# Convolution by halves of the tokens, gate products and half of the taps inside the attention, in a residual block with expert retrieval

## What is computed

```python
h = x @ w_in + b_in                # conv GLU 1024 | q, k, v 3 * 512 | gates 2 * 1024
a, gate = split(h_glu)             # branch A
c = a * sigmoid(gate)
c = causal_depthwise_conv(c, w_dw) + b_dw        # 31 taps, 512 channels
y_conv = silu(layer_norm(c)) @ w_pw2 + b_pw2
z = q @ k.T * scale                # branch B: 8 heads, strictly causal
suffix = reversed_cumsum(log_sigmoid(-z)) - log_sigmoid(-z)
y_sb = (exp(log_sigmoid(z) + suffix) @ v) @ w_o
mix = (sigmoid(g_A) * y_conv + sigmoid(g_B) * y_sb) @ w_out + b_out
x = layer_norm(alpha * x + mix)
# PEER, per token and head: two top-16 of 128 keys, top-16 of the 256 sums -> 16 expert rows
x = layer_norm(alpha * x + sum(gate * gelu(x . u[idx]) * v[idx]))
```

## Time and profile before

| | us |
|---|---|
| median of 3 runs (3281.8 to 3286.63) | 3284.27 |
| profiled execution | 3283.15 |
| its span | 3281.3 |
| first gather issued | 523.2 |
| PE, DVE, ACT, POOL busy | 2446.8, 2297.7, 1159.3, 1326.3 |
| mean granted clock of TensorE | 0.864 |

### The profile page before, as it was taken

How to read it: one execution, slowest core, us unless ns; L and a number is a source line. 1 busy time by engine, 2 the same in 40 slices (tenths; PEclk the granted TensorE clock), 3 DMA queues, 4 the chain that set the end, 5 groups by cost and what they waited for, 6 DMA issues and landing times. The chain is left out here.

```text
span 3281.3 us, 37294 instructions
## 1 busy us (share of the span) xinstructions
PE 2446.8 (75%) x12464; PEld 998.8 (30%) x12464; DVE 2297.7 (70%) x4704; ACT 1159.3 (35%) x3326; POOL 1326.3 (40%) x1197
## 2 busy tenths in 40 slices
PE   8987996778778777769899888885555555555555
PEld 7864653332223333323233332221111111111111
DVE  6986215776668888876667866666777677767775
ACT  3106112333334555533333333333333333333332
POOL 3400003344445544544343344444455445444553
PEclk9998997888888898889999999997777777777777
DMA  3101226999999999999999999999999999999997
GB/s 142 39 0 65 77 104 272 396 413 420 421 420 405 410 409 375 409 420 410 397 397 419 394 409 412 421 419 421 409 421 421 420 398 421 421 421 402 421 421 313
DMA packets 162792, 1163.71 MB, mean 355 GB/s; under 512 B 17857, under 2 KB 17985, under 8 KB 26178
## 3 DMA queue, kind: packets, MB, share of 16 engines
q0 software_dynamic: 147456, 1073.81, 79.7%
q1 hardware_dynamic: 15170, 87.79, 6.8%
HBM read 1157.33 MB, written 4.19 MB: 354 GB/s over the span
## 5 line engine op out<-in xcount | busy, mean ns | idle before, releaser
L809 PE MATMUL ps<-arena_high 64*64 64x512 f32 x8192 | 1275.3, 749 | 724.2 <-ACT arena_high L1163 721.2
L590 POOL DMA_INDIRECT arena_high<-uv_dram,idx_now x1024 | 1201.8, 1174 | 1468.7 <-PE ps L809 1269.4
L1486 DVE SCALAR_TENSOR_TENSOR arena_high<-arena_low,arena_high 128x1024 f32<-128x1024 f32 x1024 | 1237.2, 1224 | 631.4 <-DMA arena_high<-uv_dram,idx_now 620.8
L809 PEld LDWEIGHTS ps<-arena_high 64*64 64x64 f32 x8192 | 308.3, 156 | 1567.7 <-ACT arena_high L1163 1101.6
L1154 ACT ACTIVATE gcol<-hcol 128x2 f32<-128x2 f32 x512 | 103.7, 202 | 1405.8 <-DVE arena_high L1486 1403.7
L1163 ACT ACTIVATE arena_high<-arena_high,wcol 128x64 f32<-128x64 f32 x1024 | 300.4, 340 | 16.7
L1156 ACT ACTIVATE wcol<-gcol,arena_high 128x1 f32<-128x1 f32 x1024 | 245.7, 287 | 16.8
L778 PE MATMUL ps<-arena_low 128*128 128x512 f32 (+1 forms) x512 | 223.5, 580 | 0.0
L1331 DVE SCALAR_TENSOR_TENSOR arena_low<-arena_high,cols,arena_low 128x1024 f32<-128x1024 f32 x120 | 183.9, 1533 | 4.3
L585 POOL CAST idx_now<-arena_high 128x8 uint32<-128x8 f32 x128 | 59.0, 461 | 255.3 <-DVE arena_high L1472 254.7
L211 PE MATMUL ps<-x_hi_bytes,w_bytes 128*128 128x512 f32 x384 | 151.0, 393 | 0.0
(11 more groups left out here) (169 smaller groups left out, 2476.4 us busy)
## 6 DMA issues: line engine op xcount, KB each, us to landing
arena_low<-slabs_dram SPq DMA_DIRECT2D x21, 1152.0 KB
arena_high<-uv_dram,idx_now POOLq DMA_INDIRECT x1024
arena_high<-w_mix_dram SPq DMA_DIRECT2D x8, 1536.0 KB, 6.8
arena_low<-w_mix_dram SPq DMA_DIRECT2D x8, 1536.0 KB
arena_high<-w_proj_dram SPq DMA_DIRECT2D x16, 512.0 KB, 3.5
arena_high<-xT_dram SPq DMA_DIRECT2D x8, 512.0 KB, 7.7
arena_high<-w_out_dram SPq DMA_DIRECT2D x2, 2048.0 KB, 11.1
arena_high<-x_dram SPq DMA_DIRECT2D x8, 512.0 KB, 7.8
```

The costliest lines, as they stand in the source:

```text
L590: pool.indirect_dma_start(out=ring[:, s % RING, :], out_offset=None, in_=uv_d, in_offset=bass.IndirectOffsetOnAxis(ap=idx_now[:, s:s + 1], ...
L809: last = nc.tensor.matmul(ps[out_rows, bank, :], diag[rows, s % DIAGS, :], ring[rows, s % RING, cs], start=False, stop=False, skip_group_c ...
L1486: last = nc.vector.scalar_tensor_tensor(out=ring[:, s % RING, 0:D], in0=x1[c][:, j, :], scalar=1.0, in1=ring[:, s % RING, 0:D], op0=ALU.mu ...
```

## The change

Order of the projections: a and gate of all four `c`, then four q, then four k. The GLU product is split in two: the half used first goes to `conv_in`, the other with its 30 tokens of overlap is kept in `conv_in_late` for all four `c`. The taps of `h` = 1 follow at once, 512 wide; the 124 taps of `h` = 0 (`conv_tap`) stand in the attention, four behind each of the 32 `break_stick`. Mean, variance, root and swish are done per half: for `h` = 1 among the value blocks, for `h` = 0 between the branch products. Gate products (`gate_group`) stand in the attention, one of 24 matmuls in each unit, ahead of the unit's transposes; the scores of the next unit now stand behind these transposes; their sigmoids go to `mixT` and `gate_sb`. Subtraction of rounded gate weights moves from VectorE to GpSimd (`split_gates`), which does the first ahead of the attention and the other 14 in it. In the mix only branch products stay, over three pairs of PSUM banks; their weights and those of the gates are loaded apart. ScalarE rounds the value weights only when the fourth channel group's taps are done. The second half of `w_out` is loaded after the last mixed product, not the last branch product. Scores use two PSUM banks in place of four. Memory is laid out anew for all this (not shown). The core of the diff:

```diff
+            sp_eng.wait_ge(proj_done, 4 * CC)
+            load_gate(0)
+            sp_eng.wait_ge(var_done, 1)
+            load_gate(1)
             sp_eng.wait_ge(v_done, NB)
-            for m in range(2):
-                sp_eng.dma_start(w_mix[:, m, :], w_mix_d[m, :, :]).then_inc(wmix_in[m], 16)
+            load_branch(0)
+            load_branch(1)
+            for m in range(2, KD):
+                sp_eng.wait_ge(gates_done, 2 * m - 2)
+                load_gate(m)
+            sp_eng.wait_ge(gates_done, 2 * KD)
             sp_eng.dma_start(w_out_early[0], w_out_d[:, 0:CC, :]).then_inc(wout_in[0], 16)
-            for m in range(2, KD):
-                sp_eng.wait_ge(branch_done, m - 1)
-                sp_eng.dma_start(w_mix[:, m % 2, :], w_mix_d[m, :, :]).then_inc(wmix_in[m % 2], 16)
+            sp_eng.wait_ge(av_done, NU)
+            load_branch(2)
+            load_branch(3)
+            sp_eng.dma_start(b_out_bc[0], b_out_d.partition_broadcast(P)).then_inc(rows_in, 16)
+            for m in range(4, KD):
+                sp_eng.wait_ge(branch_done, m - 3)
+                load_branch(m)
+            sp_eng.wait_ge(conv_done, 2 * CC)
+            sp_eng.dma_start(x_in[0], x_d[row_of(0):row_of(0) + P, :]).then_inc(x_loaded, 16)
             sp_eng.wait_ge(branch_done, KD)
+            sp_eng.dma_start(ln1_g_bc[0], ln1_g_d.partition_broadcast(P)).then_inc(rows_in, 16)
+            sp_eng.wait_ge(mixed, KD)
             sp_eng.dma_start(w_out_early[1], w_out_d[:, CC:KD, :]).then_inc(wout_in[1], 16)
...
+            def split_gates(m):
+                for g in range(2):
+                    gs = slice(g * D, (g + 1) * D)
+                    pool.wait_ge(w_rounded, m * 2 + g + 1)
+                    nc.gpsimd.tensor_tensor(w_lo_r[:, m % 2, gs], w_gate[:, m % 2, gs], w_hi_r[:, m % 2, gs].bitcast(F32),
+                                            ALU.subtract).then_inc(w_split, 1)
+            split_gates(0)
             pool.wait_ge(v_done, NB)
             pool.memset(starts[:, P:HALF], 0.0).then_inc(starts_ready, 1)
             pool.tensor_copy(starts[:, 0:P], ident).then_inc(starts_ready, 1)
...
+            for m in range(1, KD):
+                split_gates(m)
...
+            value_block(0)
+            pe.wait_ge(conv_done, CC)
+            conv_mean(1, 4)
+            value_block(1)
+            value_block(2)
+            conv_var(1, 5)
+            for b in range(3, NB):
                 value_block(b)
...
+            def gate_group(n):
+                m, g = n // 2, n % 2
+                pe.wait_ge(w_split, n + 1)
+                if n >= 2:
+                    pe.wait_ge(sigs_ready, n - 1)
+                for k in range(KD):
+                    ws = slice(g * D + k * P, g * D + (k + 1) * P)
+                    last = split_products(ps[:, 6 + g, :], (w_hi_r[:, m % 2, ws], w_lo_r[:, m % 2, ws]),
+                                          (x_hi_r[:, 0, k, :], x_lo_r[:, 0, k, :]), k == 0, k == KD - 1)
+                last.then_inc(gates_done, 1)
             scores_of(0)
             for n in range(NU):
+                gate_group(n)
+                turn_weights(n)
                 if n + 1 < NU:
                     scores_of(n + 1)
-                turn_weights(n)
                 if n >= 1:
                     values_of(n - 1)
             values_of(NU - 1)
...
+                pe.wait_ge(wbranch_in[m % 4], (m // 4 + 1) * 16)
+                if m >= 3:
+                    pe.wait_ge(mixed, m - 2)
                 for y, src in ((0, conv_h[1]), (1, qT[1])):
                     for k in range(CC):
-                        o = 2 * D + y * HALF + k * P
-                        last = nc.tensor.matmul(ps[:, 4 * j + 2 + y, :], w_mix[:, j, o:o + P],
+                        o = y * HALF + k * P
+                        last = nc.tensor.matmul(ps[:, 2 * (m % 3) + y, :], w_branch[:, m % 4, o:o + P],
                                                 src[:, k, :], start=(k == 0), stop=(k == CC - 1))
                 last.then_inc(branch_done, 1)
+                if m == 1:
+                    pe.wait_ge(sigs_ready, 2 * KD)
+                    pe.wait_ge(conv_done, 2 * CC)
+                    conv_mean(0, 6)
+                if m == 3:
+                    conv_var(0, 7)
...
+            pe.wait_ge(std_done, 2)
...
+            def gate_out(c):
+                act.wait_ge(proj_done, 2 * c + 2)
+                if c >= 2:
+                    act.wait_ge(psum_read[2 * (c % 2)], START + 1)
+                nc.scalar.activation(glu_gate[:, c % 2, :], ps_flat[:, (4 * (c % 2) + 2) * HALF:(4 * (c % 2) + 4) * HALF],
+                                     ACT.Sigmoid, bias=cols[:, C_G + c:C_G + c + 1]).then_inc(psum_read[2 * (c % 2) + 1], 1)
+            for it in range(2):
+                next_w1(it, 0)
+                gate_out(2 * it)
+                next_w1(it, 1)
+                next_w1(it, 2)
+                gate_out(2 * it + 1)
+                next_w1(it, 3)
+            for c in range(CC):
+                act.wait_ge(proj_done, 2 * CC + c + 1)
+                nc.scalar.activation(q_both(c), halves(ps_flat[:, 2 * c * HALF:(2 * c + 2) * HALF]), ACT.Identity,
+                                     bias=q_bias8[:, c:c + 1], scale=DH ** -0.5).then_inc(psum_read[c], 1)
+                next_w1(2, c)
...
             act.wait_ge(wv_in, 16)
+            act.wait_ge(conv_done, CC)
...
+            def round_w(m):
+                act.wait_ge(wgate_in[m % 2], (m // 2 + 1) * 16)
+                for g in range(2):
...
+            round_w(0)
+            value_out(0)
+            conv_squares(1)
+            value_out(1)
+            value_out(2)
+            conv_std(1, 5)
+            value_out(3)
+            value_out(4)
+            conv_swish(1)
+            for b in range(5, NB):
...
             for hd in range(2):
                 stick_sigmoids(0, hd)
             for n in range(NU):
+                gate_sigmoid(n)
+                for hd in range(2):
+                    weights_out(n, hd)
                 for hd in range(2):
                     if n + 1 < NU:
                         stick_sigmoids(n + 1, hd)
-                    weights_out(n, hd)
+                if n % 2 == 1 and n // 2 + 2 < KD:
+                    round_w(n // 2 + 2)
                 if n % BLK == 1 and n > BLK:
                     evacuate(n // BLK - 1)
             evacuate(PAIRS - 1)
...
+            conv_squares(0)
+            conv_std(0, 7)
+            conv_swish(0)
...
+            def conv_tap(steps, c, h, k):
+                tap = c * TAPS + C_CW + k
...
+                src = src[:, PAD - k:PAD - k + HALF]
+                out = conv_h[h][:, c, :]
+                if k == 0:
+                    ins = nc.vector.tensor_scalar(out, src, cols[:, tap:tap + 1], cols[:, C_CB + c:C_CB + c + 1],
+                                                  ALU.mult, ALU.add)
+                else:
+                    ins = nc.vector.scalar_tensor_tensor(out=out, in0=src, scalar=cols[:, tap:tap + 1], in1=out,
+                                                         op0=ALU.mult, op1=ALU.add)
+                if k < TAPS - 1:
+                    steps.link(ins)
+                else:
+                    ins.then_inc(conv_done, 1)
+            taps_done = Steps(dve, conv_step)
             for c in range(CC):
-                dve.wait_ge(proj_done, c * 4 + 1)
-                dve.wait_ge(psum_read[1], START + c + 1)
-                dve.wait_ge(conv_done, START + c)
...
-                    out=conv_in[:, 0:S], in0=ps_flat[:, 0:2 * HALF], scalar=cols[:, C_A + c:C_A + c + 1],
...
-                steps = Steps(dve, conv_step, c * PAD)
...
-                steps.link(nc.vector.tensor_scalar(conv_both(c), halves(conv_in[:, PAD:PAD + S]), cols[:, tap:tap + 1],
...
-                    ins = nc.vector.scalar_tensor_tensor(
-                        out=conv_both(c), in0=halves(conv_in[:, PAD - k:PAD - k + S]), scalar=cols[:, tap + k:tap + k + 1],
...
-                ins.then_inc(conv_done, 1)
...
+                a0, j = 4 * (c % 2) * HALF, 2 * (c % 2)
+                dve.wait_ge(proj_done, 2 * c + 1)
+                dve.wait_ge(psum_read[j + 1], START + c // 2 + 1)
+                if c >= 1:
+                    dve.wait_ge(conv_done, c)
+                bias = cols[:, C_A + c:C_A + c + 1]
+                gate = glu_gate[:, c % 2, :]
+                nc.vector.scalar_tensor_tensor(out=conv_in[:, 0:HALF], in0=ps_flat[:, a0 + HALF:a0 + 2 * HALF], scalar=bias,
+                                               in1=gate[:, HALF:S], op0=ALU.add, op1=ALU.mult)
+                nc.vector.scalar_tensor_tensor(out=conv_in_late[:, c, 0:HALF + PAD], in0=ps_flat[:, a0:a0 + HALF + PAD],
+                                               scalar=bias, in1=gate[:, 0:HALF + PAD], op0=ALU.add,
+                                               op1=ALU.mult).then_inc(psum_read[j], 1)
+                dve.wait_ge(psum_read[j], START + c // 2 + 1)
```

(21 more changed lines are left out.)

237 lines of the change are left out of this document (87 added, 150 removed).

## The result

The changed kernel takes **3311.0 us** (median of 4 runs, 3303.25 to 3317.29) against 3284.6 of the kernel before on the same chip: ratio 1.0076, 95% interval 1.0058 to 1.0095. That is 26 us slower, as forecast (3310 us).

The account below looks back on a forecast made before the run. DMA gathering of experts (2758 us) bounds most; VectorE would bound the changed attention. Last mixed product 25 us late plus 1 for w_out: +26 on 3283.15 gives 3309, median 1.1 above: 3310 us, range 3286 to 3330.

Parts of the forecast that it names:

- The price of a split: Convolution taps: each GpSimd split costs VectorE 2.03 us, taken unchanged from 1024-wide taps to 512-wide ones.
- Rival 1: Convolution taps: GpSimd's lock doesn't bite half-width taps, so the kernel gets faster, 3266 us; chance 0.11.
- The projections: TensorE's order: products every 31.9 us, waits of 2.8 and 10.1 us before q groups, last group evicted at 204.2.
- sigmoid as before: Projections: the sigmoid before the first GLU product is unchanged, so product 0 is done at 38.5 us.
- a rounding of 2 us: ScalarE before the first scan: a w rounding queued ahead of table load and sigmoid, putting the scan at 271 us.
- The attention: Stick-breaking stage: VectorE sets the pace with 41.9 + 96.8 + 28.4, sum 167 us, less about 2 for overlap.
- its waits for scores are covered by the four taps: Attention: four taps (3.2 us) between two scans cover VectorE's waits for scores.
- rival 2: Attention: TensorE's low clock after gaps makes it need 181 us, 14 more than VectorE; 3324 us, chance 0.14.
- The mix: After the attention: branch groups 55.0 us, mean and variance 6.9, VectorE's last instructions; last mixed product at 502.3 us.
- Behind it: After the last mixed product: w_out's second half loads 0 to 3 us late, taken as 1.
- The first gather: Start of the expert gathering: forecast near 549 us, before the change at 523.2 us.
- The gathers: Gathering of experts: DMA-bound and touched by no edit, unchanged at 2758 us.

Follow-up runs that it names:

- memset_splits: Changed kernel with GpSimd's 14 subtractions in the attention replaced by memsets, low parts of gate weights from m = 1 left out; 3278.41 us, ratio 0.9974.
- the second profile: Profile of the changed kernel run once more with nothing edited; 3312.21 us, ratio 1.008.
- early_taps: Changed kernel with 100 of the 124 late taps moved ahead of the attention into VectorE's waits, 24 left in it; 3264.95 us, ratio 0.9936.
- gates_quarter: Changed kernel with each gate product cut from 8 to 2 input blocks, three quarters of each gate sum left out; 3312.88 us, ratio 1.0087.
- vector_slabs: early_taps with 11 of 16 w1 subtractions moved from GpSimd to VectorE and 20 taps left in the attention; 3255.41 us, ratio 0.9905.
- half_taps: early_taps with 60 taps ahead of the attention and 64 in it, two behind each stick unit; 3271.84 us, ratio 0.9958.
- vector_splits: Changed kernel with the attention's 14 gate-weight subtractions on VectorE instead of GpSimd, behind stick units of even n; 3305.81 us, ratio 1.0051.

## Why the prediction was right, and where it wasn't

**The price of a split.** The step on which all hung was to carry the 2.03 us of a 1024-wide tap over to a 512-wide one. Measured: 2.00 and 2.06 under taps, 2.02 under a scan; the twelve instructions that are held whole in the attention lose 1.95 to 2.18 us each. Rival 1 is out: no loss would be four taps in 3.11 us everywhere. By the Trainium skill (SBUF — State Buffer, section Who interferes with whom) a GpSimd instruction that reads SBUF contends with a VectorE one that has two SBUF inputs, and one that only writes doesn't; memset_splits agrees, 14 writes without a trace. Of its other statement, that the loser blocks for the whole instruction, the rows show a little less: 2.0 of 2.37 us. GpSimd pays as well: its 14 splits take 2.66 us on average in the attention (the profile is rough on GpSimd), where they take 2.37 alone.

**The projections.** Products were forecast every 31.9 us and came every 32.0, 32.0 and 31.8. The waits of the first and the third q group were forecast at 2.8 and 10.1 and are 1.5 and 9.8. The first product was forecast at 38.5, as in the kernel before, and its two halves are done at 36 us, which is most of the reason why the last group is evicted at 200.1 and not 204.2. **The step that failed** a little is "sigmoid as before". Before, the sigmoid's table load began only when TensorE's gate group was done (34.32 us), and the sigmoid at 35.61; after, the load stands at 27.71 us, ahead of the wait, and the sigmoid begins at 32.87:

```profile
27.71 1.28 ACT L1048 ACT_TABLE_LOAD   x1
32.87 1.12 ACT L1048 ACTIVATE arena_high<-ps,cols 128x1024 f32<-128x1024 f32 x1 [3.88 <-PE ps L212]
```

Of the 2.7 us, 1.3 are the table load, and 1.4 are TensorE, which is done with the group earlier in this execution; in the second profile it isn't (sigmoid at 34.49). In the code the first sigmoid has one wait ahead of it where it had two (`psum_read` and `proj_done`); that this is why the load comes earlier is my reading, and no run tells it apart. Behind the values the forecast added a rounding of 2 us to the 4.2 us from the first score to the first scan; the rounding (261.43 to 263.43 us) runs beside that score (261.68), and the time from the last value's eviction (260.93) to the first scan is 4.5 us, not 6.2. In all the first scan came at 265.5 and 269.4 us, forecast 271.

**The attention.** Forecast 167 us of VectorE's work, less 2 for overlap, so 165 from the first scan to the last; measured 166.1 and 167.6. The bound was right, and the number is so close because two errors in the sum cancel. The work itself is right: 136.7 us without the splits, forecast 138.7 less the 2. The splits were taken as 14 x 2.03 = 28.4 us, but the first two of the 14 begin ahead of the first scan:

```profile
262.55 4.76 POOL L595 TENSOR_TENSOR w_bytes<-arena_high,w_hi_bytes 128x1024 fp32r<-128x1024 f32 x2 [0.87 <-ACT w_hi_bytes L1075]
```

The first of them costs VectorE nothing and the second 1.70 us, what was left of it when the scan came (2.92 us where such a scan takes 1.22 alone). The other twelve cost 24.4 us, so it is 26 us in all. Against this stand waits of VectorE that the sum put at nothing ("its waits for scores are covered by the four taps"). By its group of waits for sigmoids in the second profile they are 36.6 - 31.5 = 5.1 us, the 31.5 being the wait before the first scan; in the first profile they are 3.8 us:

```profile
DVE arena_high L1434 <- ACT arena_high L1118: 36.6, 7, 31.5
```

Another term was mis-sized that didn't count: I gave TensorE 127 us, adding its 40.2 us of the earlier trace rows, which are at a clock of 0.84, to 87 us of gate products at full clock. With 100 taps fewer (early_taps) the attention takes 117.6 us with TensorE full, so the runs show at most 118. It left the size of the forecast alone, but my rival 2 is the worse for it: gates_quarter shows that even at a granted clock of 0.66 to 0.76 TensorE doesn't set the pace. The place that I named for it, 0.75, holds only with all of the gate products in.

TensorE's gaps have a price of their own. Its timeline, after one of the longer waits behind VectorE:

```profile
295.94 0.69 PE L704 MATMUL ps<-arena_high 128*128 128x128 f32 x2 [4.30 <-DVE arena_high L1438]
...
300.65 0.63 PE L211 MATMUL ps<-x_lo_bytes,w_hi_bytes 128*128 128x512 f32 x1
301.07 0.63 PE L212 MATMUL ps<-x_hi_bytes,w_bytes 128*128 128x512 f32 x1
...
303.48 0.39 PE L210 MATMUL ps<-x_hi_bytes,w_hi_bytes 128*128 128x512 f32 x1
```

After it the matmuls of 512 columns start every 0.43 us, the lower of the clock's two levels (1.2 GHz), and from 303 us on every 0.23 again (2.4 GHz): some 2 us lost after this gap (9 matmuls from 298.77 to 302.78 at 0.2 us more each). By the Trainium skill (TensorE: Matmul & The Clock Gate, section HAM oscillation) a kernel whose TensorE stops between bursts of matmuls pays for the low clock again after every stop; for this gap the trace agrees. But with VectorE as the bound little of it can reach the end: VectorE's waits in the attention are the 3.8 and 5.1 us above, whatever they come from.

**The mix** was forecast at 66 us from the last scan to the last mixed product (436 to 502.3) and is 66.8 (431.5 to 498.4) and 67.4; its first branch product waits for the last evictions, and VectorE for it 9.5 us. **Behind it**, w_out's second half was taken at 1 us late, between 0 and 3: the whole of both sets of products takes 15.6 us in one profile and 18.3 in the other, where it was 14.0, so 1.6 to 4.3. The wait for w_out is 1.1 to 2.5 us in the six profiles that show it; in the three up to 1.5 us the sixteen matmuls after it take 7.13 us, in the three from 2.05 us on 8.64 to 8.83. **The first gather** was forecast at 549 us and is at 545.2 and 554.3. **The gathers** were taken at 2758 us and take 2756.3 and 2758.1.

The sum came out as forecast since the errors are small and of both signs: 5.5 or 1.6 us earlier at the first scan, 1 to 2.6 later in the attention, 0.5 to 1 in the mix, 0.6 to 3.3 at w_out. That the median, 3311.0, is within 1 us of the forecast is luck: single runs of the changed kernel lie 14 us apart.

What I had not seen is the way out, although its rows stand in the prediction's own reasoning. I said of VectorE that it would be the bound, and of the stretch before the attention only where TensorE would stop there. VectorE stands idle in that stretch for 52.8 + 15.0 + 31.5 = 99 us; that is room for the very taps that the attention has none for.

## What to carry to other kernels

Work that is moved to fill one engine's gaps must be priced on every engine that it brings along: the gate products fitted into TensorE's gaps, the taps and splits put beside them made VectorE the bound by 48 us (166 against 118). Ask of a stage for the sum of each engine, take the largest as the least that it can last, and put what is over into the stretch where that engine waits; where two sums come within a few us of each other, expect more (here 8 us on 120). A GpSimd subtraction with its inputs in SBUF was paid by VectorE with 2.0 of its 2.37 us, in these rows with two SBUF inputs on both engines; whether the kernel pays depends on whether VectorE is the bound, and on VectorE the same subtraction is cheaper (1.22 against 2.03 us), if the engine that feeds it isn't late.

## What the runs showed that I had not expected

- The loss under a whole split hardly depends on VectorE's instruction: 2.03 us for a 1024-wide tap, 2.00 for a 512-wide one, 2.02 for a scan of 255 elements, which alone takes 0.69.
- Of two executions of one kernel the one is 11 us longer with no single cause: 1.6 us at the first product, 2.3 up to the first scan, 1.5 in the attention, 0.5 in the mix, 3.3 between the last mixed product and the first gather, 1.8 in the gathers. early_taps' four runs lie within 1.6 us, the changed kernel's within 14; but vector_slabs' six, with TensorE as full in the attention, lie within 13, so the tight four are no rule.
- The gather stage, which no edit touches, takes 2756.3 to 2758.3 us in four profiles of this study (before, the changed kernel twice, gates_quarter), and 2760.5 to 2767.6 in the others (memset_splits 2760.5, early_taps 2761.1, half_taps 2764.4, vector_splits 2764.8, vector_slabs 2767.6). An earlier start of the gathers doesn't explain it alone, since vector_splits' begin at 545.0 us, as in the changed kernel. The cause stays open; I made no run on it.
